# The convolutional block's up projection: its last 16 of 44 chunks as 28 chunks of seven block products each of half the width

## The reference, cut to what matters

```python
def conv_ffn(x, w_up, conv_w, conv_b, w_down):        # x 512 x 1024, w_up 1024 x 5632, w_down 2816 x 1024
    u = causal_dwconv(x @ w_up, conv_w, conv_b)       # three taps along the rows, per column
    g, val = jnp.split(u, 2, axis=-1)
    return (jax.nn.gelu(g) * val) @ w_down
```

## Time and the profile before

| | us |
|---|---|
| median of 3 executions | 1232.62 (1232.23 to 1232.89) |
| the profiled execution, its own time | 1232.7 |
| its span in the profile | 1230.8 |
| PE busy in the span | 1222.5 |
| DVE busy | 894.5 |
| ACT busy | 656.6 |

### The profile page before, as it was taken

One profiled execution on the slowest core, in us unless ns is written; L12 is line 12 of the kernel. 1 busy time (PEld: TensorE's weight loads), 2 busy tenths in 40 slices (PEclk: granted clock), 3 DMA queues, 4 the chain that ended last, 5 costly groups with the idle time before them and its releaser, 6 DMA issues.

```text
span 1230.8 us, 17188 instructions
## 1 busy us (share of the span) xinstructions
PE 1222.5 (99%) x6662; PEld 1049.8 (85%) x6662; DVE 894.5 (73%) x1277; ACT 656.6 (53%) x1085; POOL 56.1 (5%) x80
## 2 busy tenths in 40 slices
PE   9999999999999999999999999999999999999998
PEld 9877898898889888888888899778888999988886
DVE  6778888576578656655588587787685777887886
ACT  5565654244546444444556463669364544665654
POOL 0000012000000000000000000000000000000000
PEclk9999999999999999999999999999999999999999
DMA  9445578847636887878675428776727789776562
GB/s 306 140 146 177 172 275 223 273 132 194 188 103 191 209 205 240 212 227 201 211 247 180 134 70 260 205 201 179 253 90 170 263 273 262 258 224 189 172 212 79
DMA packets 63976, 244.53 MB, mean 199 GB/s; under 512 B 6900, under 2 KB 14580, under 8 KB 54424
## 3 DMA queue, kind: packets, MB, share of 16 engines
q1 hardware_dynamic: 53096, 167.55, 40.8%
q0 software_dynamic: 10368, 75.50, 24.8%
q10 hardware_dynamic: 432, 0.39, 0.1%
HBM read 235.55 MB, written 81.26 MB: 257 GB/s over the span
## 4 chain that ended last, share of the span: by engine, by line
PE 97%; DVE 2%; ACT 1%; DMA 0%; issue 0%; SPq 0%; DVEq 0%; ACTq 0%
PE bank L1518 15%; PE bank L1519 15%; PE bank L1520 15%; PE bank L1723 6%; PE bank L1724 6%; PE bank L1722 6%; PE bank L1748 3%; PE bank L1749 3%; PE bank L1750 3%; PE bank L1665 2%; PE bank L1663 2%; PE bank L1662 2%; PE bank L1667 2%; PE bank L1666 2%; PE bank L1664 2%; PE bank L1863 1%
## 5 line engine op out<-in xcount | busy, mean ns | idle before, releaser
L2507 DVE TENSOR_TENSOR wlo<-stage,whi 128x1024 fp32r<-128x1024 f32 (+1 forms) x276 | 332.8, 1212 | 114.9 <-ACT whi L1982 113.9
L1518 PE MATMUL bank<-xh,whi 128*128 128x512 f32 (+1 forms) x944 | 339.5, 360 | 0.3 <-issue 0.2
L1519 PE MATMUL bank<-xl,whi 128*128 128x512 f32 (+1 forms) x944 | 335.6, 356 | 0.0
L1520 PE MATMUL bank<-xh,wlo 128*128 128x512 f32 (+1 forms) x944 | 335.5, 355 | 0.0
L1982 ACT CAST whi<-stage 128x1024 fp32r<-128x1024 f32 (+1 forms) x276 | 284.9, 1040 | 77.8 <-PE bank L1724 27.3
L1518 PEld LDWEIGHTS bank<-xh,whi 128*128 128x128 f32 x944 | 178.5, 189 | 30.2 <-issue 5.6
L1520 PEld LDWEIGHTS bank<-xh,wlo 128*128 128x128 f32 x944 | 178.5, 189 | 25.1
L1519 PEld LDWEIGHTS bank<-xl,whi 128*128 128x128 f32 x944 | 178.6, 189 | 24.5 <-issue 0.2
L1723 PE MATMUL bank<-wlo,xh 128*128 128x512 f32 x328 | 127.8, 390 | 0.0
L1722 PE MATMUL bank<-whi,xh 128*128 128x512 f32 x328 | 127.7, 389 | 0.0
L1724 PE MATMUL bank<-whi,xl 128*128 128x512 f32 x328 | 127.7, 389 | 0.0
(11 more groups left out here) (409 smaller groups left out, 2015.1 us busy)
## 6 DMA issues: line engine op xcount, KB each, us to landing
stage<-in_W_m SPq DMA_DIRECT2D x50, 512.0 KB, 4.3
stage<-in_W_up SPq DMA_DIRECT2D x44, 512.0 KB, 4.4
m_a<-in_W_m POOLq DMA_DIRECT2D x14, 1024.0 KB, 8.0
m_b<-in_W_m POOLq DMA_DIRECT2D x14, 1024.0 KB, 8.2
stage<-in_W_in_a SPq DMA_DIRECT2D x19, 512.0 KB, 4.3
stage<-in_W_down SPq DMA_DIRECT2D x18, 512.0 KB, 4.3
stage<-in_W_out SPq DMA_DIRECT2D x16, 512.0 KB, 5.5
m_c<-in_W_m POOLq DMA_DIRECT2D x7, 1024.0 KB, 6.2
```

The source lines that it names most:

```text
L1518: e.matmul(b[:, cols], hi[:, k, :], xh[:, k, cols], start=(k == 0), stop=False)
L1519: e.matmul(b[:, cols], hi[:, k, :], xl[:, k, cols], start=False, stop=False)
L1520: last = e.matmul(b[:, cols], lo[:, k, :], xh[:, k, cols], start=False, stop=(k == 7))
L2507: e.tensor_tensor(wlo[:, plan.place[i], c], stage[:, i % NSTAGE, c], whi[:, plan.place[i], c].bitcast(F32), ALU.subtract).then_inc(S["w_lo"])
```

## The change

The last 16 chunks of `up` (eight gate and eight value tiles) become four groups of seven chunks, by the scheme of `m1`: 56 chunks of `up` in place of 44. Eight additions and subtractions on DVE and four splits (`x_sum` with three kept places, then `r4`) make the input sums during the plain chunks. 16 more transfers make the sums of `w_up`'s blocks, so that there are 88; `at` spreads them anew: four in the first mixer's input projection, ten from `kv_k` on, ten at `xq`, 27 during `up`, and the eight for kind `d` of `m2` during `m2`. The functions `m1_...` of the block products become `feat_...` for both layers. The early split of `down`'s first inputs after half of the last `up` chunk (`LAST_X`) goes. Buffers move: `v`, `w` of `up` lie at 64 to 72 KB of R, a second gate buffer at 72 KB, and two of `down`'s sum buffers at 92 and 94 KB.

```diff
-           ("xq", 8), ("xo", 8), ("up", 44), ("down", 34), ...
+           ("xq", 8), ("xo", 8), ("up", 56), ("down", 34), ...
-GROUPS = {"down": 4, "m1": 6, "m2": 8}
+GROUPS = {"up": 4, "down": 4, "m1": 6, "m2": 8}
+UP_PLAIN = 2 * NF1 - 4 * GROUPS["up"]
+ORDER = [o for o in ORDER if (o[0], o[2][0]) != ("m2", "d")] + [o for o in ORDER if (o[0], o[2][0]) == ("m2", "d")]
...
     def conv_ffn(self):
         self.step("up_setup")
-        for j in self.feat("up", 2 * NF1):
-            if j == 2 * NF1 - 1:
-                self.seven_ahead("down")
+        self.up_x = self.x
+        for j in self.feat("up", UP_PLAIN):
             self.step("up", j // 2, j % 2)
...
+            if 8 <= j < 12:
+                self.combine("up", ("t21", "t22", "t11", "t12")[j - 8])
+            elif 12 <= j < 16:
+                self.combine("up", ("r1", "r3", "r2", "r4")[j - 12])
+            elif j == 17:
                 self.seven_first("down")
+            elif UP_PLAIN - 4 <= j < UP_PLAIN - 1:
+                self.sum_kept("up", ("r2", "r1", "r3")[j - UP_PLAIN + 4])
+        for i, (kind, g) in enumerate(FEATS["up"]):
+            self.up_seven(i, kind, g)
...
+    def feat_seven(self, name, i, kind, g, last):
+        if kind not in NEW_BANK:
+            self.fill(name, g, kind)
+        self.need()
+        self.step("seven_feat", name, i)
+        self.used += 1
+        if kind in ("r1", "r2", "r3") and g == last:
+            self.give((name, kind), "mm", CHUNK0[name] + PLAINS[name] + i + 1)
+
+    def up_seven(self, i, kind, g):
+        last = GROUPS["up"] - 1
+        self.feat_seven("up", i, kind, g, last)
+        if kind == "r2":
+            self.copy("up", "taken", g)
+            self.step("feat_taken", "up", g)
+            if g == 0:
+                self.step("x_sum", "up", "r4")
+                self.x_split("up", "r4")
+            else:
+                self.pump()
+                self.up_done(g - 1)
+        elif kind == "t11":
+            self.combine("up", "v", g)
+        elif kind == "r1":
+            self.combine("up", "w", g)
+            self.out(("up", g, "r1"), "combined", self.combined)
+            self.copy("up", "seed", g)
+            self.step("feat_seed", "up", g)
+        elif kind == "r3":
+            self.combine("up", "c22", g)
+            self.combine("up", "c21", g)
+        else:
+            if (kind, g) == ("t22", last):
+                self.seven_ahead("down")
+            n = ("t12", "r4", "t22").index(kind)
+            self.pump()
+            self.step("up_quarter", n, g)
+            self.out(("up", g, ("t11", "r2", "r3")[n]), "up_u", UP_PLAIN + 3 * g + n + 1)
+            if n:
+                self.step("up_y", g, 2 - n)
+            if n == 2:
+                self.step("up_taps", g, 1)
+                if g == last:
+                    self.up_done(g)
+        self.pump()
+
+    def up_done(self, g):
+        self.step("up_taps", g, 0)
+        self.step("up_gelu", g)
+        self.step("up_mult", g)
+        c = UP_PLAIN // 2 + 2 * g + 2
+        if c % 4 == 0 and c <= 4 * GROUPS["down"]:
+            self.combine("down", "r1", c // 4 - 1)
+            self.combine("down", "r3", c // 4 - 1)
...
             def at(n):
-                if n < 9:
+                if n < 4:
+                    return CHUNK0["in_a"] + 4 + 3 * n
+                if n < 14:
                     return CHUNK0["kv_k"]
-                if n < 17:
-                    return CHUNK0["xq"] + n - 8
-                if n < 43:
-                    return CHUNK0["up"] + 2 + 8 * (n - 17) // 5
-                if n < 61:
-                    return CHUNK0["in2_c"] + 1 + (n - 43)
-                if n < 64:
-                    return CHUNK0["m1"] + 3 + 2 * (n - 61)
-                return CHUNK0["m1"] + PLAIN + 2 + 4 * (n - 64)
+                if n < 24:
+                    return CHUNK0["xq"] + n - 13
+                if n < 51:
+                    return CHUNK0["up"] + 2 + 19 * (n - 24) // 10
+                if n < 69:
+                    return CHUNK0["in2_c"] + 1 + (n - 51)
+                if n < 72:
+                    return CHUNK0["m1"] + 3 + 2 * (n - 69)
+                if n < 80:
+                    return CHUNK0["m1"] + PLAIN + 2 + 4 * (n - 72)
+                return CHUNK0["m2"] + 1 + 4 * (n - 80)
...
+            add_up(0, 4)
             for h in range(4):
                 rs = st[:, 120 + 32 * (h % 2):124 + 32 * (h % 2)]
                 q.wait_ge(S["ml_set"], 2)
                 q.wait_ge(S["ml_rv"], h + 1)
                 e.tensor_tensor(rs, rs, mhalf, ALU.pow).then_inc(S["ml_rs"])
-                add_up(2 * h, 2 * h + 2)
-            add_up(8, len(ORDER))
+                add_up(4 + 2 * h, 6 + 2 * h)
+            add_up(12, len(ORDER))
```

223 lines of the change are left out of this document (139 added, 84 removed).

## The result

The changed kernel takes 1250.74 us (median of four executions, 1246.79 to 1255.12) against 1232.74: a ratio of 1.0148, 95% interval 1.0136 to 1.0161. It is slower, by 18 us, and outside the predicted range of 1229 to 1241. Its executions spread over 8 us where those of the kernel before spread over 0.7. The profiled one took 1255.12 (span 1253.3) and is the slowest of the four, so the profile shows 22.5 us more than the span of before, and some of what it shows is that execution's own.

A forecast was written before the change was run, and what follows sets the result against it. The prediction took PE to bound the kernel (97% of the chain). Against 1232.7 us it summed -6.4 (TensorE) + 5.4 (DVE's queue and `down`) + 3.3 (loads) + 1.0 (POOL) + 0.3 (moved rows) = +3.6, so 1236.3 us, range 1229 to 1241.

The forecast's parts named there:

- TensorE: `up`: 16 plain chunks of 5.44 us replaced by 28 block chunks of 2.88, gaining 6.40 us.
- DVE's order in the groups: New groups of `up`: PE waits for late `v` and `c21`, 1.3 in group 1, 0.2 in 2, 2.4 in 3.
- `down`'s start: Hand-over from `up`: DVE's leftover work makes `down`'s fifth input late, a PE wait of 1.5 us.
- The price of a wait: Whole kernel: a wait of PE costs its full time, its own length.
- Late loads: New groups: landings of 5.2 us, 0.8 late behind groups 1 and 2, 1.7 in 3; 3.3 us, ends 0 and 7.
- POOL's chain: First mixer: additions delay the last `pow` and so `out1`; 1.0 us taken, range 0 to 2.4, at worst 3.9.
- the moved rows: After the first mixer: transfers running on to about 249 cross rows with 0.45 us slack; 0.3 us, ends 0 and 1.
- Rival (c): DMA saturates: landings of 6.4 all through, loads cost 7, last `pow` at its worst 3.9; 1243.6 us, chance 10%.
- Rival (b): Groups: DVE uses waits behind ACT, `v` ahead of time, only group 3's splits and `down`'s start cost; 1228.3 us, 18%.
- the signs that the prediction named: Profile after: 2.88 a chunk, PE idle before `t12` and `t22`, `down`'s fifth chunk late, ACT awaiting loads in groups 2 and 3.

The follow-up runs named there:

- e10: e6 with nearly all of the groups' taps on DVE left out as well (8 of 512 columns stay): 1227.96 us, ratio 0.9966 to the kernel before.
- e6: e5 with 16 of the 24 transfers for `m1` left out, its chunks loading plain weights instead: 1239.74 us, ratio 1.0058 to the kernel before.
- e1: Changed kernel with the 13 summing transfers beside the 28 block chunks of `up` moved into `down`'s chunks: 1245.52 us, ratio 1.0101 to the kernel before.
- e5: Changed kernel with early transfers retimed off the moved rows (four three chunks earlier, two additions held until `xq`): 1249.82 us, ratio 1.0163 to the kernel before.
- the four corners: Four runs with e5's early front: full taps 1249.8 us, 16 transfers out 1239.7, light taps on DVE 1237.1, both 1228.0.
- e11: e6 with `v` ahead of old taps, a split ahead of the seed, `down`'s inputs ahead of waiting casts, kept places back last: 1234.59 us, ratio 1.0017.
- e8: e7's queue order with all 88 transfers, five beside the 28 block chunks and eight in `down`: 1245.04 us, ratio 1.0108 to the kernel before.
- e12: e11's queue order with all 88 transfers, 3 beside the 28 chunks, 2 in `down`, more beside plain chunks, others pushed back: 1254.51 us, ratio 1.0170.
- e2: Changed kernel with `v` put ahead of the previous group's gate taps, gelu, products and `down` sums: 1251.52 us, ratio 1.0155 to the kernel before.
- e7: e6 with `v` first, a split ahead of the seed, kept places back after the last `c21`, `down`'s inputs ahead of value taps: 1236.14 us, ratio 1.0034.
- f4: e11's order with two groups, four plain `up` chunks behind them, 80 transfers, `LAST_X` split back: 1233.64 us, ratio 1.0009 to the kernel before.
- f6: e11's order with four groups, four plain `up` chunks behind them, all 88 transfers, `LAST_X` split back: 1243.06 us, ratio 1.0083 to the kernel before.

## Why the prediction was wrong

**TensorE: right.** From 531.60 to 560.39 ten block chunks take 28.79 us, 2.88 each. e10 shows the gain as time.

**DVE's order in the groups: right in place and size.** Predicted 1.3 in group 1, 0.2 in group 2, 1.2 at `v` and 1.2 at `c21` in group 3, 3.9 in all. In e6, with few late loads, 1.53, none, 1.24 and 1.04, 3.8 in all; e1 has the same, 1.52, none, 1.23 and 1.02. The timeline of DVE in group 1 of the changed kernel has the order that was counted, with `down`'s two sums (L3213, L3215) ahead of `v` (L3153):

```profile
564.11 0.69 DVE L3213 TENSOR_TENSOR R<-R 128x512 f32<-128x512 f32 x1
564.72 0.69 DVE L3215 TENSOR_TENSOR R<-R 128x512 f32<-128x512 f32 x1
565.32 0.68 DVE L3153 TENSOR_TENSOR R<-R,bank 128x512 f32<-128x512 f32 x1
```

**`down`'s start: mis-sized.** Predicted 1.5, at the fifth input. e6 has 2.08 there, and 1.35 at the second input, which the prediction didn't price: ACT's queue holds it behind the copy of the `t22` step and two casts, which waited 1.73 and 0.46 us for loads even here. `down` loses 5.6 us in e6 in all.

**The price of a wait: missing.** A wait of PE was priced at its own length. In e6 PE waits 7.2 us in the groups and `down`, and these stretches are 10.6 us too long. Of the 3.4 us between, 1.5 are matmuls at the lower clock behind the wait of 2.08 (granted clock 0.57 from 626.73 to 629.80); the rest is about 0.2 at each wait that a row's idle time leaves out, and a few smaller ones. The lower clock doesn't follow every wait. In the traces of the runs here it follows each of the 17 waits of 3.3 to 7.7 us in the block chunks and `down`, 11 of the 21 between 1.8 and 2.8, and none of the 30 between 0.9 and 1.6.

**Late loads: the step that failed.** The prediction took 5.2 us for a landing, between the medians of the earlier trace rows, and 3.3 us for the term, with 7 as its upper end, all of it inside the groups and nothing at `down`'s start. Measured, the transfers cost 10.1 us, and in the profiles of e5 and e6 6.1 of 9.9 fall into `down`. The loads of the 28 chunks, issue to landing:

```profile
DMA to landing us min/median/max: 3.3/6.4/11.5
```

The median is that of the additions in the earlier trace rows, the longest is above it. The chain of the changed kernel in group 3 shows what one such load does:

```profile
594.76 2.36 DVE wlo L2597 x2
597.14 11.47 DMA stage<-in_W_up
...
615.28 0.28 DVE R L3153
```

Two extra splits empty two buffers and their loads go out at 596.01 and 597.14. The first lands after 3.8 us, the second after 11.47; the cast, the split, four taps, a gelu and the products follow, and `v` is 5.28 us late. What lies between the two is POOL's addition, issued at 596.35. The DMA view of 597 to 606.3, with issue to landing as the last number:

```profile
m_b<-in_W_m POOLq DMA_DIRECT2D x1, 1024.0 KB, 12.1
stage<-in_W_up SPq DMA_DIRECT2D x1, 512.0 KB, 11.5
stage<-up_d SPq DMA_DIRECT2D x1, 512.0 KB, 10.9
stage<-down_a SPq DMA_DIRECT2D x1, 512.0 KB, 9.1
stage<-down_c SPq DMA_DIRECT2D x1, 512.0 KB, 6.3
```

Issued at 596.35, 597.14, 599.01, 601.99 and 606.02, they land at 608.4, 608.6, 609.9, 611.1 and 612.4: the loads come in behind the addition, one after the other. A second such piece (621.79, 9.16 us) makes `down`'s second input 6.21 late:

```profile
628.66 1.05 ACT L2045 CAST whi<-stage 128x1024 fp32r<-128x1024 f32 x1 [6.51 <-DMA stage<-down_a]
...
633.96 1.64 ACT L2082 CAST xh<-R 128x512 fp32r<-128x512 f32 x3
```

Against e6 the loads are worth 9.0 us in the groups and 3.9 in `down`, 12.9 in this profile, but this sets the slowest execution against the fastest; between the medians of e5 and e6 it is 10.1. The error was to let loads enter by a median. What a load takes goes by how much is left of the transfer that is under way when it is issued. In the traces of all runs here, counting every load of a weight chunk behind 260 us (4636), issue to landing is:

| when the load is issued | loads | min / median / max us |
|---|---|---|
| no 1 MB transfer until it lands | 1488 | 3.0 / 4.1 / 7.0 |
| the same, two or more other loads under way | 337 | 3.1 / 4.5 / 7.0 |
| 3 to 5 us left of a transfer | 613 | 4.2 / 5.6 / 11.8 |
| 5 to 7 us left | 485 | 3.1 / 7.2 / 10.5 |
| more than 7 us left | 594 | 3.4 / 8.5 / 12.1 |

The low ends of the last two rows are loads issued just behind the transfer itself: of the 257 that were issued within 0.5 us of it, 178 landed more than 1 us ahead of it; of the 822 issued later, none did. Loads that go out together are not late by themselves. The kernel before shows it already. The longest landing of the earlier trace rows, issued at 1040.72, ends 0.6 us behind an addition issued at 1038.52 (DMA view of 1038.4 to 1050):

```profile
m_d<-m_c POOLq DMA_DIRECT2D x1, 1024.0 KB, 11.2
stage<-m_a SPq DMA_DIRECT2D x1, 512.0 KB, 9.6
```

The prediction did see that group 3's splits empty the stage (its 1.7), but priced it by the same 5.2.

The rule of the Trainium skill that the prediction cited ("DMA: Bandwidth & Descriptors", section Queues, rings and completion order: a DMA engine alternates between queues packet by packet) gives no time of its own, and the traces do not look like an even sharing: a load half as large as the transfer should then land well ahead of it (an estimate from the rule and the two sizes), and these land with it or behind it. Why is not shown. That the transfers hurt in the groups only where DVE has no slack is shown by the four corners.

**POOL's chain: harmless, the moved rows not.** The last `pow` started at 205.28, ahead of the predicted 206.5 to 209, and was over by 206.95, ahead of the 208.7 that it may end at; PE waited 0.24 us ahead of the second chunk of `out1`; 1.0 had been taken. The copy at 117.12 made PE wait 1.1 us for the turned rows, a place that the prediction didn't look at. The moved rows were priced at 0.3, ends 0 and 1, for a slack of 0.45; measured, the projection behind them begins 3.7 us later than before. 1.1 of this had been lost by the second chunk of `out1`, so 2.7 are theirs, and the projection's 192 matmuls take 1.3 us more behind the waits. With the 1.1 before and 0.4 ahead of `up` these are the 5.5 of the front in this execution; by the medians of the changed kernel and e5 it is worth 0.9 or less.

**The sum.** Predicted -6.4 + 5.4 + 3.3 + 1.3 = +3.6. Measured in the profile -6.4 + 10.6 (DVE's order and the matmuls behind its waits) + 12.9 (loads) + 5.5 (front) - 0.2 = +22.4, against 22.5 between the spans; it holds for the slowest execution, and its two middle terms rest on the profile of e6's fastest. The medians, each against the kernel before in its own series, give +18.0 (after), +17.7 (e5), +7.7 (e6) and -4.3 (e10), so: TensorE's gain with what is lost even then -4.3, the taps on DVE +11.9, the transfers +10.1, the front +0.3. By this count DVE's term (5.4) is as far off as that of the loads (3.3), through the price of a wait, `down`'s second input and its fifth; where the 11.9 fall is not shown in full, since the two profiles differ by 8.4 in the groups and `down`.

Rival (c), the DMA saturates, came nearest with 1243.6. Its landings, 6.4 at the median, were right, but 7 us for the loads were too few, and its 3.9 on POOL's chain came to 0.24. Rival (b), DVE uses the waits, had group 2 right and fell with group 1 of e6, where `v` was late by 1.53. Of the signs that the prediction named, 2.88 a chunk and the waits ahead of `t12` came; there was no wait ahead of `t22` in the changed kernel, not the fifth but the second input of `down` was late, and ACT waited for loads in group 0 (2.55) as well as in groups 2 and 3.

**Still open.** Why executions of one kernel spread over 2 to 11 us was not settled; the boundary after `out1` explains part of it, but e5 without that part spreads as much, and so does e11 (9.4), which has no transfer beside the last three groups. Where a load falls in a transfer's time may explain more; no run tested it. What makes the clock fall behind one wait of 1.8 to 2.8 us and not behind another is open too.

## What to carry to other kernels

Before cutting matmuls out of a stage, count the queue that feeds it at the new cadence: here DVE went from 57% of the stage (49.8 of 87.0 us) to 86% of what the block chunks should take (69.5 of 80.6), and from there on a late load could no longer be caught up. Price a load not by the median landing but by what is left of the large transfer under way when it is issued: here up to 11.5 us, where the median was 6.4, and ask which result that PE wants stands behind it in ACT's and DVE's queues. Where transfers can't be moved out of the way (e1, e8 and e12 moved them and paid elsewhere), their cost is part of the change that needs them. Reordering a nearly full queue moved the waits (from `v` to the seed in e2, from inputs to a split in e7 and e11) and gave back at most 5 us (e11 against e6). Four plain chunks behind the groups took two of the waits away and left a third (f4 to f6), so no version got the whole gain.

## What the runs showed of the hardware

A load of 512 KB from HBM landed after 3.0 to 7.0 us without a transfer of 1 MB from HBM to HBM under way, however many other loads were, and with or just behind such a transfer where it was issued more than 0.5 us behind its issue; in the 28 chunks that made 3.3 to 11.5 us. Eight moves of 128 KB between SBUF regions took 4.2 us at the median beside such an addition where they took 2.6 in the kernel before. Behind a wait of PE of 2.49 us matmuls of 256 columns started 0.21 us apart at a granted clock of 0.51 for 3 us and then 0.12 apart again; behind a wait of 2.72 the granted clock stayed at 1.00. In the changed kernel's groups and `down` 17.1 us of waits cost PE 23.6 us.
